# Gathering expert rows in one hybrid encoder block: one 8 KB fetch per row pair, or two of 4 KB into two rings

## What is computed

```python
def peer_ffn(x, w_query, sub_keys, u_table, v_table):
    q = (xt @ w_query).reshape(t, PEER_HEADS, 2, PEER_HALF)
    s = jnp.einsum('thpd,hpnd->thpn', q, sub_keys)
    s_top, i_top = lax.top_k(s, PEER_TOPK)
    ...
    expert = idx1 * PEER_KEYS + idx2
    gate = jax.nn.softmax(c_top, axis=-1)
    def block(args):
        xb, eb, gb = args
        u = u_table[eb]
        hid = jax.nn.gelu(jnp.einsum('td,thkd->thk', xb, u), approximate=False) * gb
        return jnp.einsum('thk,thkd->td', hid, v_table[eb])
```

## Time and profile before

| what | value |
|---|---|
| median of the runs | 4269.25 us (4261.28 to 4270.88) |
| the profiled execution, from its first to its last instruction | 4275.2 us |
| first issue of a gather in it | at 1445.5 us |
| last issue of a gather in it | at 4243.6 us |
| gathers | 1024 of 1 MB |
| PE, DVE, ACT, POOL busy, share of the span | 84%, 65%, 35%, 31% |
| mean granted clock of TensorE | 0.933 |

### The profile page before, as it was taken

The page is one execution under the profiler, slowest core; times in us unless marked ns, Lnnn a source line. Parts: engine busy times, 40 slices in busy tenths (PEclk is TensorE's granted clock), DMA queues, the critical chain, the costliest instruction groups (busy, mean ns, idle before and its releaser), DMA issues.

```text
span 4275.2 us, 51141 instructions
## 1 busy us (share of the span) xinstructions
PE 3611.6 (84%) x12032; PEld 1999.4 (47%) x12032; DVE 2783.4 (65%) x7483; ACT 1497.8 (35%) x4117; POOL 1340.5 (31%) x1182
## 2 busy tenths in 40 slices
PE   7999979999799788787888888788888888888776
PEld 4666757777544433333333343333333333334332
DVE  1566667777611576777767676767777676767664
ACT  3333344444322233333333333333333333333333
POOL 1000000000011244444444444444444444444333
PEclk9999989999699899999999999999999999999888
DMA  3110010000100599999999999999999999999998
GB/s 99 31 30 20 1 39 20 29 29 20 73 31 25 205 373 398 387 384 388 376 393 374 409 379 388 393 375 389 396 396 383 389 387 395 377 403 379 373 360 326
DMA packets 197497, 1135.42 MB, mean 266 GB/s; under 512 B 18240, under 2 KB 60352, under 8 KB 64704
## 3 DMA queue, kind: packets, MB, share of 16 engines
q0 software_dynamic: 147456, 1073.81, 61.9%
q1 hardware_dynamic: 49984, 60.97, 4.2%
HBM read 1130.52 MB, written 4.19 MB: 265 GB/s over the span
## 4 chain that ended last, share of the span: by engine, by line
PE 21%; DMA 17%; issue 13%; POOL 8%; ACT 4%; DVE 1%; POOLq 1%; ACTq 0%; DVEq 0%; SPq 0%
PE peer_ps_o L1334 15%; DMA peer_ring<-in_table,peer_index_odd 9%; DMA peer_ring<-in_table,peer_index_even 9%; POOL peer_ring L1294 8%; PE peer_ps_q L1310 5%; ACT peer_diag L1390 1%; ACT peer_hid L1384 1%; PE peer_ps_s L1319 1%; ACT peer_act_out L1380 1%; ACT peer_qs L1346 1%; DVE peer_junk L1523 0%; ACT L1380 0%; ACT peer_gate_now L1375 0%; POOLq L1292 0%; POOLq L1293 0%
## 5 line engine op out<-in xcount | busy, mean ns | idle before, releaser
L1334 PE MATMUL peer_ps_o<-peer_ring,peer_diag 128*128 128x512 f32 x4096 | 1999.5, 644 | 511.9 <-ACT peer_diag L1390 511.8
L1523 DVE SCALAR_TENSOR_TENSOR peer_junk<-peer_ring,Y 128x1024 f32<-128x1024 f32 x1024 | 1254.3, 1225 | 617.8 <-ACT peer_diag L1390 202.1
L1334 PEld LDWEIGHTS peer_ps_o<-peer_ring,peer_diag 128*128 128x128 f32 x4096 | 818.1, 206 | 1653.9 <-issue 930.6
L1294 POOL DMA_INDIRECT peer_ring<-in_table,peer_index_even x512 | 620.7, 1212 | 772.0 <-PE peer_ps_o L1334 681.8
L1294 POOL DMA_INDIRECT peer_ring<-in_table,peer_index_odd x512 | 619.6, 1210 | 766.3 <-PE peer_ps_o L1334 653.4
L1380 ACT ACTIVATE peer_act_out<-peer_dots 128x2 f32<-128x2 f32 x512 | 103.1, 201 | 1333.7 <-DVE peer_junk L1523 1333.0
L1390 ACT ACTIVATE peer_diag<-ident,peer_hid 128x128 f32<-128x128 f32 x1024 | 355.2, 394 | 21.6
L1310 PEld LDWEIGHTS peer_ps_q<-hnT,wq 128*128 128x128 f32 x2048 | 243.9, 196 | 31.6 <-issue 31.5
L1384 ACT ACTIVATE peer_hid<-peer_act_out,peer_gate_now 128x1 f32<-128x1 f32 x1024 | 245.7, 287 | 16.7
L1310 PE MATMUL peer_ps_q<-hnT,wq 128*128 (+1 forms) x2048 | 244.6, 279 | 1.9 <-SPq L94 1.9
L360 PE MATMUL ssd_ps_piece<-hnT,w_group 128*128 128x512 f32 x512 | 229.8, 602 | 6.9 <-ACT ssd_raw L444 5.1
(11 more groups left out here) (233 smaller groups left out, 3891.7 us busy)
## 6 DMA issues: line engine op xcount, KB each, us to landing
w_group<-in_w_ssd SPq DMA_DIRECT2D x16, 512.0 KB, 4.2
mo_w<-in_w_out SPq DMA_DIRECT2D x4, 2048.0 KB, 15.0
wq<-in_w_query SPq DMA_DIRECT2D x8, 1024.0 KB, 9.1
peer_ring<-in_table,peer_index_even POOLq DMA_INDIRECT x512, 11.4
peer_ring<-in_table,peer_index_odd POOLq DMA_INDIRECT x512, 11.6
hg_w<-in_w_hg SPq DMA_DIRECT2D x14, 512.0 KB, 4.2
hg_w<-in_w_hg SPq DMA_DIRECT2D x7, 1024.0 KB, 5.9
w_group<-in_w_ssd SPq DMA_DIRECT2D x4, 1040.0 KB, 5.9
```

The lines of the kernel that those rows point to most:

```text
L1294: pool.indirect_dma_start(ring[:, k % RING, :], None, table, bass.IndirectOffsetOnAxis(ap=index_now[:, k:k + 1], axis=0)).then_inc(got[k % ...
L1334: mm = nc.tensor.matmul(ps_o[:, half, :], diag[:, k % RING, :], ring[:, k % RING, D + half * 512:D + (half + 1) * 512], start=(k == 0), st ...
L1523: nc.vector.scalar_tensor_tensor(out=junk[:], in0=ring[:, s, 0:D], scalar=1.0, in1=Y[:, bass.ds(b, 1), D:MIX].rearrange("p o d -> p (o d)" ...
```

## The change

The table is no longer put together: u and v stay separate tables with rows of 4 KB. Each pair is fetched by two indirect DMAs of 512 KB, one into `ring_u` and one into `ring_v`, of 8 slots each. POOL waits before the u fetch for a new semaphore `read_slots`, that DVE raises after each dot, and before the v fetch for `free_slots`, that PE raises as before. DVE waits for u's landing alone, PE for v's. DVE has one more wait, for its own dot, before it raises `read_slots`. To have semaphores enough, the 19 semaphores of `input_norm` are cleared on SP's queue at the start of `ssd`.

```diff
-        ring = sb("ring", [P, RING, 2 * D])
+        ring_u = sb("ring_u", [P, RING, D])
+        ring_v = sb("ring_v", [P, RING, D])
...
             pool.sem_inc(free_slots, RING)
+            pool.sem_inc(read_slots, RING)
...
                 for k in range(TOPK):
+                    pool.wait_ge(read_slots, n * TOPK + k + 1)
+                    pool.sem_inc(pool_turn, 1)
+                    pool.indirect_dma_start(ring_u[:, k % RING, :], None, u_rows,
+                                            bass.IndirectOffsetOnAxis(ap=index_now[:, k:k + 1], axis=0)
+                                            ).then_inc(got_u[k % RING], 16)
                     pool.wait_ge(free_slots, n * TOPK + k + 1)
                     pool.sem_inc(pool_turn, 1)
-                    pool.indirect_dma_start(ring[:, k % RING, :], None, table,
+                    pool.indirect_dma_start(ring_v[:, k % RING, :], None, v_rows,
                                             bass.IndirectOffsetOnAxis(ap=index_now[:, k:k + 1], axis=0)
-                                            ).then_inc(got[k % RING], 16)
+                                            ).then_inc(got_v[k % RING], 16)
...
                     pe.wait_ge(diag_ready, past(n * TOPK + k + 1))
+                    pe.wait_ge(got_v[k % RING], (n * 2 + k // RING + 1) * 16)
...
-                    dve.wait_ge(got[s], (n * 2 + k // RING + 1) * 16)
+                    dve.wait_ge(got_u[s], (n * 2 + k // RING + 1) * 16)
...
                         op0=ALU.mult, op1=ALU.mult, accum_out=dots[:, k:k + 1]).then_inc(dot_ready, 1)
+                    dve.wait_ge(dot_ready, past(n * TOPK + k + 1))
+                    dve.sem_inc(read_slots, 1)
...
             sp.dma_start(pr[:], par).then_inc(par_in, 16)
+            for s in spent:
+                sp.sem_clear(s)
             for kt in range(KT):
                 sp.dma_start(first_weights(Y, kt), w_hg[0, :, kt, :]).then_inc(head_in, 16)
```

More of the change, by code:

```diff
@@ L147, in sb @@
             return ctx.enter_context(nc.sbuf_tensor("nrm_" + name, shape, dt))
-        primed = []
+        primed, spent = [], []
         def plain_sem(name):
-            return ctx.enter_context(nc.semaphore("nrm_" + name))
+            spent.append(ctx.enter_context(nc.semaphore("nrm_" + name)))
+            return spent[-1]
         def sem(name):
@@ L229, in _ @@
                 mm.then_inc(turned, 1)
+    return spent
 def first_weights(Y, kt):
@@ L241, in first_piece, with ssd @@
     return Y[:, KT // 2 + 2 + half, D + (p - 2) * 2 * P:D + (p - 1) * 2 * P]
-def ssd(nc, w, w_in, w_ssd, par, w_hg, C, hnT, Y):
+def ssd(nc, w, w_in, w_ssd, par, w_hg, C, hnT, Y, spent):
     with ExitStack() as ctx:
@@ L1160, in _, with peer @@
             dve.wait_ge(kept, past(NB))
-def peer(nc, w_query, keys, table, fin_w, C, Y, xnT, wq, wq_in, out):
+def peer(nc, w_query, keys, u_rows, v_rows, fin_w, C, Y, xnT, wq, wq_in, out):
     with ExitStack() as ctx:
@@ L1221, in peer @@
         ps_o = psum("ps_o", [P, 2, 512])
-        got = [plain_sem(f"got{s}") for s in range(RING)]
+        got_u = [plain_sem(f"got_u{s}") for s in range(RING)]
+        got_v = [plain_sem(f"got_v{s}") for s in range(RING)]
+        read_slots = plain_sem("read_slots")
         counted = sem("counted")
@@ L1332, in gather @@
                     pe.wait_ge(diag_ready, past(n * TOPK + k + 1))
+                    pe.wait_ge(got_v[k % RING], (n * 2 + k // RING + 1) * 16)
                     for half in range(2):
                         mm = nc.tensor.matmul(ps_o[:, half, :], diag[:, k % RING, :],
-                                              ring[:, k % RING, D + half * 512:D + (half + 1) * 512],
+                                              ring_v[:, k % RING, half * 512:(half + 1) * 512],
                                               start=(k == 0), stop=(k == TOPK - 1))
@@ L1523, in gather @@
                     nc.vector.scalar_tensor_tensor(
-                        out=junk[:], in0=ring[:, s, 0:D], scalar=1.0,
+                        out=junk[:], in0=ring_u[:, s, :], scalar=1.0,
                         in1=Y[:, bass.ds(b, 1), D:MIX].rearrange("p o d -> p (o d)"),
                         op0=ALU.mult, op1=ALU.mult, accum_out=dots[:, k:k + 1]).then_inc(dot_ready, 1)
+                    dve.wait_ge(dot_ready, past(n * TOPK + k + 1))
+                    dve.sem_inc(read_slots, 1)
                 if route_next:
@@ L1535, in _, with block_program @@
             finish(NB - 1)
-def block_program(nc, x, ln_w, w_ssd, par, w_hg, lb_logits, w_out, mix_w, ffn_w, w_query, keys, table, fin_w, out):
+def block_program(nc, x, ln_w, w_ssd, par, w_hg, lb_logits, w_out, mix_w, ffn_w, w_query, keys, u_rows, v_rows, fin_w, out):
     with ExitStack() as ctx:
@@ L1548, in block_program @@
                 group_in = [sems.enter_context(nc.semaphore(f"group_in{i}")) for i in range(len(SSD_PARTS))]
-                input_norm(nc, x, ln_w, w_ssd, C, hnT, w_group, group_in)
-                ssd(nc, w_group, group_in, w_ssd, par, w_hg, C, hnT, Y)
+                spent = input_norm(nc, x, ln_w, w_ssd, C, hnT, w_group, group_in)
+                ssd(nc, w_group, group_in, w_ssd, par, w_hg, C, hnT, Y, spent)
             hgrn(nc, w_hg, lb_logits, C, hnT, Y, osq, ysq)
@@ L1554, in block_program @@
         mix_out(nc, x, w_out, mix_w, ffn_w, w_query, C, Y, osq, ysq, hnT, wq, wq_in)
-        peer(nc, w_query, keys, table, fin_w, C, Y, hnT, wq, wq_in, out)
+        peer(nc, w_query, keys, u_rows, v_rows, fin_w, C, Y, hnT, wq, wq_in, out)
 def laid_out(inputs):
@@ L1592, in laid_out @@
         "keys": first("sub_keys").transpose(3, 0, 1, 2).reshape(P, PH * 2 * KEYS),
-        "table": np.concatenate([first("u_table"), first("v_table")], 1),
+        "u_rows": first("u_table"),
+        "v_rows": first("v_table"),
         "fin_w": np.broadcast_to(np.asarray(inputs["ln_final_w"]), (P, D)),
```

## The result

The changed kernel takes 4358.92 us (median of four runs, 4346.84 to 4369.53) beside 4267.06 us for the kernel before on the same chip: a ratio of 1.0202, with a 95% interval of 1.0173 to 1.0232. It is slower, by 92 us where 163 were forecast.

What follows compares the result with a forecast made beforehand. Transfers bound the kernel before, with a hole per block; POOL's doubled issues would bound it after: 40.5 + 5.8 = 46.3 us a block against 43.75, times 64, is 163 us more: 4432 us on the median, range 4245 to 4640.

Steps and rivals of the forecast that it cites:

- The 40.5 us without any wait: POOL's row for a block: 32 issues of 0.94 us plus 0.30 gap, and 0.8 for the index copy.
- The waits at DVE: POOL's issues held up by DVE instructions: 5.8 us a block, 0.18 per issue, with ends 0 and 8.7 us.
- dots that had waited for a landing: POOL's waits at the 8 of 16 dots paced by landings: 0.45 us each, 3.6 us a block.
- the other dots: POOL's waits at some 8 dots following each other at 1.27 us: 0.1 us each, 0.8 us a block.
- the two products of the experts' part: POOL's issues stretched by two DVE products in the routing: 0.7 us each, 1.4 us a block.
- With POOL late it gives nothing: u slot returned by the dot: u runs ahead one fetch at most, 1.27 us per border; no gain with POOL late.
- Transfers of 4 KB rows: Gathers on the DMA engines: 41.35 us a block become 42.3, covered by POOL; uncovered, 1.0 us a block.
- The fixed part of a transfer: 2.0 us per fetch beyond issue and transfer, costing nothing as long as several fetches are in flight.
- The forecast DMA share: DMA engines' share in the gathers' stage: about 0.91, without the border hole; still 1.0 mid-block would show the prediction wrong.
- Rival 1: POOL and DVE fall into step, transfers stay the bound: 22 to 93 us faster, about 4215 us; 12%, unchanged time 7%.
- Rival 2: Both fetches of a pair wait at dots: 50.4 us a block, +425, about 4700 us; 7%.
- Rival 3: Each transfer's fixed 2.0 us is paid once more per pair, the queue holding one fetch: about 6300 us; 1%.

Runs made afterwards that it cites:

- run 2: Changed kernel with u and v rows cut to 512 columns, half the bytes, dots and matmuls reading each half row twice: 4421.73 us, 1.0347.
- run 3: Changed kernel with dots over the first 64 columns only, the rest of each dot left out: 4166.07 us, 0.9747 to the kernel before.
- run 4: Kernel before the change with its dots over 64 columns instead of 1024: 4177.59 us, 0.9779.
- run 5: Changed kernel with DVE copying each block's activations to PSUM at the block's start, so dots read one operand there: 4273.00 us, 0.9992.
- run 9: Changed kernel in which POOL waits before each u fetch for free_slots as well as read_slots: 4384.41 us, 1.0257.
- run 6: Changed kernel with dots' second operand in PSUM, DVE copying it for the next block ahead of its wait for PE's last matmul: 4212.97 us, 0.9860.
- run 7: Kernel before (one table, 8 KB rows) with activations copied to PSUM ahead of the block's last wait, dots reading them there: 4253.47 us, 0.9951.
- run 1: Changed kernel with one small memset more on POOL between each pair's u and v fetch: 4360.32 us, 1.0205.
- run 10: Changed kernel with four memsets of 128x16 on POOL behind each u fetch: 4794.74 us, 1.1224.
- run 8: Changed kernel without read_slots: u fetch waits for PE's release, v fetch for nothing more, DVE neither waits for its dot nor raises a count: 4745.82 us, 1.1119.
- run 12: Changed kernel with dots' second operand in PSUM, copied by ACT at the start of its block instead of by DVE: 5076.36 us, 1.1887.

## Why the prediction was right

**The mechanism held.** POOL became the bound, its idle time ended by "issue" and not by PE, without the stop at the border, and busy for 53% of the span, as forecast. Runs 2 to 5 show that it is POOL and not the transfers, and what stretches its issues.

**The sum, term by term, for a block.** The issue of half the columns was taken as 0.94 us, and the median is 0.94; the gap as 0.30, and it is. The 40.5 us without any wait stand. The waits at DVE were put at 5.8 us, 0.18 per issue. The mean of the four groups is 1.071 us, so they are 0.13 per issue, or 4.2 us. This is the step that was mis-sized, and its three parts were off both ways. In the changed kernel's trace 870 issues take longer than 0.97 us, and all but one end 0.8 us behind the end of a dot or of a product of the experts' part, so that each wait can be laid to one of them:

| waits of POOL, us a block | forecast | measured |
|---|---|---|
| dots that had waited for a landing | 3.6 | 2.0 (328 issues, 0.38 each) |
| the other dots | 0.8 | 2.2 (539 issues, 0.26 each) |
| the two products of the experts' part | 1.4 | 0.02 (2 issues) |

The first part was taken nearer to no step at all (0.62 us) than to full step (0.1), and the engines keep step more than that. The second took the step of 1.27 us between two dots from the kernel before, but the change's own wait and semaphore step behind each dot make it 1.46. An issue that follows one released by a dot's end then waits some 0.2 us for the end of the next dot, as the one at 2447.30 above. By these rows DVE's new wait, priced as free because DVE has time to spare, is paid on POOL; no run takes it away with all else kept. The third took the 0.7 us from the kernel before, where an issue meets the second product in 60 of 64 blocks. In the changed kernel the last dot holds an issue, and the next one starts just where the first product ends (2608.25) and the second begins, and isn't held:

```profile
2605.87 1.23 DVE L1537 SCALAR_TENSOR_TENSOR peer_junk<-peer_ring_u,Y 128x1024 f32<-128x1024 f32 x1 [1.54 <-DMA peer_ring_u<-in_u_rows,peer_index_odd]
2606.69 1.22 POOL L1307 DMA_INDIRECT peer_ring_v<-in_v_rows,peer_index_even  x1 [0.30 <-issue]
...
2607.26 0.99 DVE L1489 TENSOR_TENSOR peer_hit<-peer_count,peer_placef 128x800 f32<-128x800 f32 x1 [0.15 <-DVE peer_junk L1537]
...
2608.21 0.94 POOL L1302 DMA_INDIRECT peer_ring_u<-in_u_rows,peer_index_even  x1 [0.30 <-issue]
2608.29 0.99 DVE L1491 TENSOR_TENSOR peer_hit<-peer_hit,peer_expert 128x800 f32<-128x800 f32 x1
```

That the sum came within 1.6 us of the measured one is thus in part luck: the errors are -1.6, +1.4 and -1.4 us. Beyond these there are 0.3 us of waits over the gap for PE's slots and DVE's queue: 40.5 + 4.2 + 0.3 = 45.0, which is what the issues' times give. The block of before was put at 43.75 us, but 2798 us over 64 blocks are 43.72. The excess over it was put at 2.55 us a block and is 1.33, which is 85 us in 64 blocks. Between the two profiled executions the span grew by only 70 us, as the changed kernel starts its gathers 5 us earlier and ends 10 us sooner behind its last issue. The medians are 92 us apart, and the runs of one kernel spread over 10 to 23 us.

**"With POOL late it gives nothing"** (the early u slot): nearly. It gives 25 us (run 9), 0.4 us a block; POOL does come up against PE's slots now and then.

**Transfers of 4 KB rows** were put at 42.3 us a block, and covered. Uncovered, with short dots, a block of the two tables is 42.1 us by the issues' times, and 402 GB/s are moved. The price was right within 0.2 us. **The fixed part of a transfer** overlaps: with landings of 6.2 us (4 to 6 forecast, 11.5 before) and an issue every 1.4 us, four to five fetches are under way. Breaking the Trainium skill's rule (DMA: Bandwidth & Descriptors, "Bandwidth") to batch to 1 MiB has no cost here: run 6 with fetches of 512 KB beats run 7 with 1 MB. The formula of 2.0 us plus bytes / 436e3 that the prediction names beside it stands in that page's section "Anatomy of one DMA — SWDGE (gpsimd) path"; it is for one DMA, and no sum here rests on it.

**The forecast DMA share** of 0.91 was wrong: 0.99 was measured. The prediction had named a share still at 1.0 in the middle of a block as a sign that it was wrong, and the sign came (1.03 from 2400 to 2424 us) though POOL was the bound. The forecast took the packets' time to be that of the full stream, 1.024 times the 41.35 us of before. But the page's 65.1% of 4345.1 us is 2829 us, 1.07 times the 2646 us of before, while with short dots (65.4% of 4164.8 us) it is 2724, or 1.03 times. So the packets take more time in all where POOL sets the pace than where they flow at 402 GB/s; why is not shown. The share isn't a measure of how near the rate is to its limit: 0.99 goes with 376 GB/s here, 1.01 with 424 before, and half the bytes (run 2) still give 0.64.

**Rival 1** (the transfers remain the bound, 4215 us) has its condition in the POOL waits: under 2.9 us a block. They were 4.2. Runs 5 and 6 took them away, down to 0.3 and 0.4 us a block, and in run 6 the rival's time came, 4213 us. Of this, 21 us are what the kernel before gains by the PSUM operand alone (0.5%, run 7), and the 40 us beside that one lie in the rival's 22 to 93. It was the nearest rival, and its price held. The Trainium skill's sentence for it (SBUF — State Buffer, "Who interferes with whom"), that `tensor_tensor` was not seen to stall a DMA, isn't borne out here: the issue inside the `tensor_tensor` L1477 took 1.63 us, and in run 5 the issues that still wait do so for such products. What the same section says of a DVE instruction with two SBUF inputs, that it contends with a GpSimd instruction that reads SBUF, fits: the mean issue takes 1.07 us with dots from SBUF and 0.95 with one operand in PSUM. **Rival 2** (two waits per pair) came in single pairs (1.16 for u and 1.62 for v in the timeline above), never as a state: a block took 45.0 us and not 50.4. **Rival 3** (about 6300 us) was far off.

## What to carry to other kernels

An engine that is idle two thirds of the time can still become the bound by a change that doubles its instructions: count its row for a block (instructions times their usual duration, plus the gap between them) before looking at its busy share. A wait added to an engine with time to spare can be paid by the engine that runs in step with it. The price of an indirect DMA of 128 rows on POOL did not go by the bytes in a row (a median of 0.94 us for 8 KB and for 4 KB, 0.95 for 2 KB), so splitting a row costs a full issue. Whether it goes by the number of rows no run tested. And if DVE runs long instructions with two operands in SBUF beside such issues, put one operand in PSUM: the copy of 1.2 us per 16 uses turned a loss of 2.0% into a gain of 1.4%, once it stood where DVE waited anyway.

## What the runs showed of the hardware

**Small work on POOL fits behind an indirect DMA.** Behind an issue POOL idles 0.30 us. A memset of 0.12 us goes into it and the next issue starts no later (run 1); four of them cost 0.13 us net (run 10).

**PE can come late for no reason that the profile names.** In three kernels (runs 8, 10 and 12) the score products, normally 0.65 us behind the last query product, come a median of 3.8, 4.2 and 7.9 us behind it. In the other eleven traces, of the two kernels and the other nine runs, the median is 0.65 us. PE's part of the program is the same in the changed kernel and in these three runs. Between the two stands ACT's copy of the query products. It begins a median of 3.2, 3.6 and 7.4 us behind the last query product that the trace records, where it is 0.12 us in the changed kernel, then takes its usual 0.38, and the scores follow 0.15 later. So what comes late is the signal of the query products, not ACT's work. In run 12 the delay is partly seen among the query products themselves (PE's timeline):

```profile
2405.98 3.18 PE L1325 MATMUL peer_ps_q<-hnT,wq 128*128 x27
2410.18 0.27 PE L1325 MATMUL peer_ps_q<-hnT,wq 128*128 x1 [1.03 <-issue]
2411.59 0.37 PE L1325 MATMUL peer_ps_q<-hnT,wq 128*128 x1 [1.14 <-issue]
...
2415.81 0.37 PE L1325 MATMUL peer_ps_q<-hnT,wq 128*128 x1 [1.03 <-issue]
2418.16 1.22 PE L1334 MATMUL peer_ps_s<-peer_kT,peer_qs 128*128 x4 [1.98 <-ACT peer_qs L1362]
```

In the changed kernel all 32 run through, and the scores follow:

```profile
2433.47 3.73 PE L1323 MATMUL peer_ps_q<-hnT,wq 128*128 x32
2437.87 0.71 PE L1332 MATMUL peer_ps_s<-peer_kT,peer_qs 128*128 x4 [0.67 <-ACT peer_qs L1360]
```

The five last query products come 1.4 us apart with nothing waited for, where all 32 take 3.73 us otherwise. The mean granted clock of these runs is lower (0.87 from 1500 to 4100 us in run 8, 0.85 in run 10, 0.80 in run 12, beside 0.92 in the changed kernel); how much of the loss that makes is not shown. Whether it has to do with how PE gets its instructions no run tests, and the pages give no support for it: the instruction queue q14 carried 36 packets in run 8, as in the kernel before, and 68 and 67 in runs 10 and 12, beside 67 in the changed kernel. What sets it off stays open: run 10 has only an edit on POOL, run 8 one on POOL and DVE, run 12 one on ACT and DVE, and the kernel of run 9, whose u fetches wait for PE as in run 8, doesn't have it. So before an experiment's time is laid to its edit, the gap between two instructions that the edit doesn't touch should be looked at.
